# Two kernel edits in a fused stack of mixers: the second half of the down product in other PSUM banks, and the final norm placed ahead of the overflow branch

## What is computed

```python
def swiglu_2(h, w_gate, w_up, w_down):
    a = jnp.einsum("bsd,df->bsf", h, w_gate)
    u = jnp.einsum("bsd,df->bsf", h, w_up)
    return jnp.einsum("bsf,fd->bsd", jax.nn.silu(a) * u, w_down)
...
def second_block(x, mem, ...):
    for l in range(DEPTH):
        ...
        h = rmsnorm_2(x, norm_ffn_w[l])
        if l % 2 == 0:
            x = x + swiglu_2(h, ffn_w_gate[j], ffn_w_up[j], ffn_w_down[j])
        else:
            x = x + moe_swiglu(h, router_w[j], moe_w_gate[j], moe_w_up[j], moe_w_down[j])
    return rmsnorm_2(x, norm_final_w)
```

## Time and profile before

| | us |
|---|---|
| Median of 3 runs | 2752.84 |
| Lowest and highest | 2751.36, 2758.93 |
| The profiled execution, its own time | 2753.78 |
| Its span, from first to last instruction | 2752.0 |
| TensorE busy | 2533.3 |
| VectorE busy | 1757.8 |
| ScalarE busy | 1479.8 |

### The profile page before, as it was taken

The page is one execution under the profiler, slowest core; times in us unless marked ns, Lnnn a source line. Parts: engine busy times, 40 slices in busy tenths (PEclk is TensorE's granted clock), DMA queues, the critical chain, the costliest instruction groups (busy, mean ns, idle before and its releaser), DMA issues.

```text
span 2752.0 us, 42814 instructions
## 1 busy us (share of the span) xinstructions
PE 2533.3 (92%) x17242; PEld 2240.5 (81%) x17242; DVE 1757.8 (64%) x2362; ACT 1479.8 (54%) x1894; POOL 28.0 (1%) x85
## 2 busy tenths in 40 slices
PE   4987799999998789989888999988999999999997
PEld 3865579999997479989688998877788888888886
DVE  3245956545454575546465546556788988988886
ACT  3225545434442564545555435554677777777775
POOL 0000000000000000001000001000000000000000
PEclk8998899999999799999899999999999999999998
DMA  7251415545543164545133455222799999999994
GB/s 275 93 199 61 184 62 199 184 169 184 184 146 143 48 245 169 184 153 185 48 138 139 183 183 172 108 95 106 273 357 349 352 357 353 351 357 352 351 355 181
DMA packets 81580, 566.00 MB, mean 206 GB/s; under 512 B 9265, under 2 KB 12593, under 8 KB 13553
## 3 DMA queue, kind: packets, MB, share of 16 engines
q1 hardware_dynamic: 80096, 559.95, 54.7%
q0 software_dynamic: 1296, 3.38, 0.5%
HBM read 559.92 MB, written 1.05 MB: 204 GB/s over the span
## 4 chain that ended last, share of the span: by engine, by line
PE 82%; DVE 9%; ACT 5%; issue 2%; DMA 1%; SPq 0%; PEldq 0%; DVEq 0%; ACTq 0%
PE psum L232 81%; DVE ring_lo L226 2%; ACT ring_hi L223 1%; PE psum L641 1%; DMA ring<-in_stream 1%; DVE hT L718 1%; PE psum L1829 1%; ACT hT L682 1%; DVE hT L429 1%; DVE Z L1191 1%; ACT Z L690 1%; ACT L415 0%; DVE Z L1165 0%; DVE Z L1164 0%; DVE h_lo L439 0%
## 5 line engine op out<-in xcount | busy, mean ns | idle before, releaser
L226 DVE TENSOR_TENSOR ring_lo<-ring,ring_hi 128x2048 fp32r<-128x2048 f32 x479 | 1096.9, 2291 | 478.4 <-ACT ring_hi L223 475.5
L223 ACT ACTIVATE ring_hi<-ring 128x2048 fp32r<-128x2048 f32 x479 | 916.3, 1914 | 391.0 <-PE psum L232 388.3
L232 PE MATMUL psum<-a_hi,ring_hi 128*128 128x256 f32 (+1 forms) x2448 | 733.0, 299 | 59.7 <-DVE h_lo L437 20.0
L232 PE MATMUL psum<-a_hi,ring_lo 128*128 128x256 f32 (+1 forms) x2448 | 727.0, 297 | 0.0
L232 PE MATMUL psum<-h_lo,ring_hi 128*128 128x256 f32 (+1 forms) x2128 | 629.6, 296 | 0.0
L232 PEld LDWEIGHTS psum<-a_hi,ring_hi 128*128 128x128 f32 x2448 | 476.8, 195 | 77.8 <-issue 43.4
L232 PE MATMUL psum<-ring_hi,a_hi 128*128 128x512 f32 (+1 forms) x1680 | 520.9, 378 | 5.9 <-DVE h_lo L437 3.7
L232 PEld LDWEIGHTS psum<-a_hi,ring_lo 128*128 128x128 f32 x2448 | 476.2, 195 | 10.3
L232 PEld LDWEIGHTS psum<-h_lo,ring_hi 128*128 128x128 f32 x2128 | 415.4, 195 | 7.6
L232 PEld LDWEIGHTS psum<-ring_hi,a_hi 128*128 128x128 f32 x1680 | 313.5, 189 | 58.2 <-issue 4.1
L232 PE MATMUL psum<-ring_lo,a_hi 128*128 128x512 f32 (+1 forms) x976 | 353.3, 362 | 0.0
(11 more groups left out here) (257 smaller groups left out, 2395.7 us busy)
## 6 DMA issues: line engine op xcount, KB each, us to landing
ring<-in_stream SPq DMA_DIRECT2D x529, 1024.0 KB, 4.9
mixT<-mixT POOLq DMA_DIRECT2D x32, 71.0 KB, 5.6
cst<-in_constants SPq DMA_DIRECT2D x1, 1216.0 KB, 14.9
xT<-in_xT SPq DMA_DIRECT2D x1, 1024.0 KB, 9.6
xT<-in_ctxT SPq DMA_DIRECT2D x1, 1024.0 KB, 11.9
xT<-in_memT POOLq DMA_DIRECT2D x1, 1024.0 KB, 6.1
out_y<-hT SPq DMA_DIRECT2D x1, 1024.0 KB, 4.8
Z<-in_level_masks SPq DMA_DIRECT2D x1, 448.0 KB, 15.3
```

Of the source, the lines that this page charges most:

```text
L223: e.activation(hi, raw, ACT.Copy).then_inc(sem("piece_rounded"), 1)
L226: e.tensor_tensor(lo, raw, hi.bitcast(F32), ALU.subtract).then_inc(sem("piece_split"), 1)
L232: ins = pe.matmul(*args, **kw)
```

## The change

Two edits. In the dense feed-forward runs, `ups` and `downs` choose the banks: in runs 0, 2 and 3 the up product stays in banks 0 to 3, half 0 of the down product in 4 to 7, and half 1 goes to 0 to 3; in run 1 all is swapped. The wait for `down_added` goes, and the means that follow some runs move from bank 0 to bank 4. At the end, the last norm is called by each engine ahead of the first `phase_end` behind the experts (and once more inside the branch), the squares are taken two tiles at a time as `e_x_added` rises, the second `phase_end` goes, and the output is stored in two DMAs.

```diff
-        def act_last_norm(act):
-            act_squares(act, 0, T)
-            act_rms(act, 0, 0, T)
-
-        def dve_last_norm(dve):
-            await_next(dve, "inverse_rms")
+        rs_last = hT[:, 0, T:2 * T]
+
+        def pe_last_norm(pe, pre):
             for k in range(KT):
-                dve.scalar_tensor_tensor(hT[:, k, 0:T], xT[:, k, 0:T], v("final2", 0, k, k + 1), mixT[:, 0, 0:T],
-                                         ALU.mult, ALU.mult)
+                if k % 2 == 0:
+                    pe.wait_ge(sem("last_squared"), 4 * (pre == "o") + k // 2 + 1)
+                mm(pe, bank[2][:, 0:T], const("mean"), hT[:, k, 0:T], start=k == 0, stop=k == KT - 1,
+                   last_of="last_mean" if k == KT - 1 else None)
+
+        def act_last_norm(act, pre):
+            act.preload_act_table_set("natural_log")
+            for b in range(4):
+                act.wait_ge(sem(pre + "_x_added"), N_EXP * 4 + b + 1)
+                act.activation(hT[:, 2 * b:2 * b + 2, 0:T], xT[:, 2 * b:2 * b + 2, 0:T], ACT.Square)\
+                   .then_inc(sem("last_squared"), 1)
+            act.wait_ge(sem("last_mean"), 1 + (pre == "o"))
+            link(act, act.activation(rs_last, bank[2][:, 0:T], ACT.Ln, bias=EPS))
+            act.activation(rs_last, rs_last, ACT.Exp, scale=-0.5).then_inc(sem("last_root"), 1)
+
+        def dve_last_norm(dve, pre):
+            dve.wait_ge(sem("last_root"), 1 + (pre == "o"))
+            for k in range(KT):
+                ins = dve.scalar_tensor_tensor(hT[:, k, 0:T], xT[:, k, 0:T], v("final2", 0, k, k + 1), rs_last,
+                                               ALU.mult, ALU.mult)
+                if k % 4 == 3:
+                    ins.then_inc(sem("y_ready"), 1)
...
+        def ups(run):
+            return bank[4:8] if run == 1 else bank[0:4]
+
+        def downs(run, half):
+            return bank[0:4] if (run == 1) != (half == 1) else bank[4:8]
+
...
-                    mm(pe, bank[2 * (f % 2) + half][:, 0:T], w[wp][:, k * 256 + half * P:k * 256 + (half + 1) * P],
+                    mm(pe, ups(run)[2 * (f % 2) + half][:, 0:T], w[wp][:, k * 256 + half * P:k * 256 + (half + 1) * P],
...
                 for d in range(4):
-                    if f == 0 and half == 1:
-                        pe.wait_ge(sem("down_added"), run * 8 + d + 1)
                     for i, (wp, ap) in enumerate(THREE):
                         last = f == FT - 1 and i == 2
-                        mm(pe, bank[4 + d][:, 0:T], w[wp][:, (q % 4) * 512 + d * P:(q % 4) * 512 + (d + 1) * P],
+                        mm(pe, downs(run, half)[d][:, 0:T], w[wp][:, (q % 4) * 512 + d * P:(q % 4) * 512 + (d + 1) * P],
...
-                    ps, x = bank[4 + q % 4][:, 0:T], xT[:, q, off:off + T]
+                    ps, x = downs(run, half)[q % 4][:, 0:T], xT[:, q, off:off + T]
...
-            sp.wait_ge(sem("y_ready"), 1)
-            sp.dma_start(y_out, hT[:, :, 0:T]).then_inc(sem("y_stored"), 16)
-            sp.wait_ge(sem("y_stored"), 16)
+            for half in range(2):
+                sp.wait_ge(sem("y_ready"), half + 1)
+                tiles = slice(4 * half, 4 * half + 4)
+                sp.dma_start(y_out[:, tiles, :], hT[:, tiles, 0:T]).then_inc(sem("y_stored"), 16)
+            sp.wait_ge(sem("y_stored"), 32)
...
                     pe_experts(pe, "e", 0)
+                    pe_last_norm(pe, "e")
                     phase_end(pe)
                     with pe.If(pe.value_load(overflow[0:1, 0:1], min_val=0, max_val=1) > 0):
                         pe_experts(pe, "o", N_EXP // 2)
+                        pe_last_norm(pe, "o")
                     pe.nop()
-                    phase_end(pe)
-            pe_norm(pe, 0, T)
```

More of the change, by code:

```diff
@@ L546, in act_ffn @@
                         act.wait_ge(sem("hidden_full"), run * FT + f - 1)
-                    act.activation(mixT[:, f % 2, 0:T], bank[2 * (f % 2)][:, 0:T], ACT.Silu)\
+                    act.activation(mixT[:, f % 2, 0:T], ups(run)[2 * (f % 2)][:, 0:T], ACT.Silu)\
                        .then_inc(sem("silu"), 1)
@@ L567, in dve_ffn @@
                     dve.wait_ge(sem("silu"), run * FT + f + 1)
-                    dve.tensor_tensor(hid(f, 1, Z), mixT[:, f % 2, 0:T], bank[2 * (f % 2) + 1][:, 0:T], ALU.mult)\
+                    dve.tensor_tensor(hid(f, 1, Z), mixT[:, f % 2, 0:T], ups(run)[2 * (f % 2) + 1][:, 0:T], ALU.mult)\
                        .then_inc(sem("hidden_full"), 1)
@@ L1988, in act_two_norms @@
             await_next(act, "mean_of_normed")
-            act.activation(rs_two[:, 0:T], bank[0][:, 0:T], ACT.Ln, bias=EPS)
+            act.activation(rs_two[:, 0:T], bank[4][:, 0:T], ACT.Ln, bias=EPS)
             link(act, act.activation(rs_two[:, T:2 * T], rs_two[:, T:2 * T], ACT.Ln, bias=EPS * EPS))
@@ L1996, in dve_two_norms @@
             await_next(dve, "two_means")
-            link(dve, dve.tensor_scalar(rs_two[:, T:2 * T], bank[0][:, 0:T], EPS, None, ALU.mult))
-            dve.tensor_tensor(rs_two[:, T:2 * T], rs_two[:, T:2 * T], bank[0][:, T:2 * T], ALU.add)\
+            link(dve, dve.tensor_scalar(rs_two[:, T:2 * T], bank[4][:, 0:T], EPS, None, ALU.mult))
+            dve.tensor_tensor(rs_two[:, T:2 * T], rs_two[:, T:2 * T], bank[4][:, T:2 * T], ALU.add)\
                .then_inc(sem("mean_of_normed"), 1)
@@ L2098, in _ @@
                         load(r * SLOTS + (n_pieces + s - again), (n_pieces + s) % SLOTS)
+                sp.wait_ge(sem("y_ready"), 4)
             sp.nop()
-            sp.wait_ge(sem("y_ready"), 1)
-            sp.dma_start(y_out, hT[:, :, 0:T]).then_inc(sem("y_stored"), 16)
-            sp.wait_ge(sem("y_stored"), 16)
+            for half in range(2):
[3 more added lines that the diff above has]
+            sp.wait_ge(sem("y_stored"), 32)
         @block.tensor
@@ L2126, in _ @@
                 else:
-                    pe_mean(pe, 0, (3, 4, 5, 6, 7), 0, 2 * T, "two_means")
+                    pe_mean(pe, 4, (3, 4, 5, 6, 7), 0, 2 * T, "two_means")
             for layer in range(DEPTH):
@@ L2145, in _ @@
                     pe_ffn(pe, 3)
-                    pe_mean(pe, 0, (3, 4, 5, 6, 7), 0, T)
+                    pe_mean(pe, 4, (3, 4, 5, 6, 7), 0, T)
                 else:
@@ L2194, in _ @@
                 else:
-                    act_rms(act, 0, 0, T)
+                    act_rms(act, 4, 0, T)
                     act_apply(act, [b2_segment("norm_mix", 1)])
@@ L2222, in _ @@
                     act_experts(act, "e", 0)
+                    act_last_norm(act, "e")
                     phase_end(act)
@@ L2225, in _ @@
                         act_experts(act, "o", N_EXP // 2)
+                        act_last_norm(act, "o")
                     act.nop()
-                    phase_end(act)
-            act_last_norm(act)
         @block.vector
@@ L2300, in _ @@
                     dve_experts(dve, "e", 0)
+                    dve_last_norm(dve, "e")
                     phase_end(dve)
@@ L2306, in _ @@
                         dve_experts(dve, "o", N_EXP // 2)
+                        dve_last_norm(dve, "o")
                     dve.nop()
-                    phase_end(dve)
-            dve_last_norm(dve)
-            dve.drain().then_inc(sem("y_ready"), 1)
         @block.gpsimd
```

## The result

| | us |
|---|---|
| Kernel before, median of 4 runs | 2754.06 (2751.36 to 2758.93) |
| Changed kernel, median of 4 runs | 2729.23 (2728.85 to 2732.19) |
| Ratio, changed to before | 0.991, 95% interval 0.9893 to 0.9927 |
| Changed kernel, profiled execution and its span | 2729.36 and 2727.5 |

The change made the kernel faster, by 0.7 to 1.1%. The spans of the two profiled executions differ by 24.5 us.

What follows compares the result with a forecast made beforehand. TensorE, busy 2533.3 of 2752.0 us, was taken to bound the kernel; 8.9 + 3.4 + 9.4 = 21.7 us off the 2752.84 median gave some 2731 us, own range 2726 to 2737, 8 in 10 within 2725 to 2739.

Steps and rivals of the forecast that it cites:

- the predicted 21.7 us: Whole kernel: 8.9 from the middles' waits, 3.4 from the clock behind them, 9.4 from the end.
- 8.9 + 3.4: Dense runs' middles: four TensorE waits of 2.2 us go, and two clock falls of 1.7 us behind them.
- the second claim: Middles: the gain stays, with no later wait for a split; the rival that it is given back had 0.08.
- The lead of 7.3 us: Half 1 of the down product: the next piece is split at 566.9 and wanted at 574.2.
- The end, 9.4: Last norm and store: VectorE ends 9.2 us sooner, TensorE's branch ends last; the gain is 9.4 us.
- 5.1 (4.7 + 0.4): Program end: 4.7 us from VectorE's end to TensorE's drain behind the branch, then 0.4 to the span's end.
- the end costs more: Rival at the end: branch beside the store takes twice, or mean at low clock; 3 to 3.6 us, chance 0.10.
- Storing in two halves alone is worth nothing while the branch is last: Output store: it hides behind TensorE's later branch, so splitting it gains 0 by itself.
- the bound of 10.7: End: upper gain of 10.7 us if the branch costs little, as on ScalarE (45 ns), and the store ends it.
- the trace agrees on ScalarE: Overflow branch: the skill's 0.11 us per compare-and-branch was said to fit ScalarE's 45 ns, not TensorE's 3.63 us.
- the way in which the forecast could fail: Other short stretches: a shift of all work by some us can add or remove a few clock falls.

Runs made afterwards that it cites:

- the first edit alone: Kernel before with only the new banks for the down product and no waits on its additions, end as before: 2737.63 us, ratio 0.9938.
- one store: Changed kernel with a single store of all of hT instead of two; one profiled execution, 7.7 us from VectorE's end to the span's end.
- the two kernels with the new table set: Changed kernel with natural_log_exp_and_others preloaded instead of natural_log: 2712.78 us; the same with phase_end also moved into the overflow branch: 2713.27 us.
- the kernel with the additions first: Kernel before with VectorE's four additions at the middle written ahead of that step's piece split, banks and waits kept: 2739.37 us, ratio 0.9943.
- the two short branches: Changed kernel with a nop instead of the overflow pass: with two stores 3.4 us from VectorE's end to the span's end, with a single store 5.2.
- the early branch: Changed kernel with the phase_end behind the last norm moved into the branch, so TensorE branches right behind its mean products: 2727.75 us, ratio 0.9904.
- the one with new banks: Changed kernel with the four waits on the down product's additions put back, its banks kept: 2745.63 us.
- edit 2: Kernel before with only the last norm ahead of the branch and the two stores, the four waits kept: 2745.24 us, ratio 0.9965.

## Why the prediction was right

**The size.** Forecast 2731, measured 2729.2. Of the predicted 21.7 us the runs gave 12.3 + 9.0 = 21.3 in the two places that were named, and 3.1 more elsewhere in the profiled execution. The medians differ by 24.8 us and not 21.7. That the forecast still lies within 2 us is luck for 1.2 us of it: with a fourth run the median of the kernel before is 2754.06, and I had subtracted from 2752.84.

**The middles, 8.9 + 3.4.** Both terms are right in kind, and 12.3 was measured between the splits, though two small errors cancel in it. An interval with a fall of the clock is 9.6 us and one without is 8.0 to 8.15, so a fall costs 1.5 us, where I had 1.7, and without the falls the pauses cost some 9.3 us, where I had 8.9. That nothing is given back later was the second claim, and the first edit alone shows it. The lead of 7.3 us was more than enough; I did not try how little would do.

**The end, 9.4.** It gave 9.0. The mean took 3.62 us (I had 3.7) at the clock of 1.00. VectorE's end to the span's end was 5.7 us where I had 5.1 (4.7 + 0.4): the flag's load took 0.79 instead of 0.49 us and the branch 4.02 instead of 3.63, both while the store moved. Of the branch's part little is sure: with the DMA engines idle it took 3.4 to 3.9 us. So the rival "the end costs more" was right in its mechanism and took at most 0.6 us, not 3 to 3.6.

**One step was wrong.** "Storing in two halves alone is worth nothing while the branch is last" treated branch and store as independent. The fetch behind the branch shares the DMA engines with the store: with one store the branch takes 2.3 us longer, and the two halves are worth 2.0 us.

**A row misread.** I took the 45 ns of the earlier trace rows as the branch's cost on ScalarE and built the bound of 10.7 on it. ScalarE did nothing for 2.5 us behind that row, so it doesn't show a cheap jump over the long body, and my sentence that the trace agrees on ScalarE doesn't hold for the whole jump. A cheap one is shown only with the short body, 0.24 us on TensorE. The sum did not use it.

**The clock elsewhere.** I named it as the way in which the forecast could fail. It made the kernel faster than my sum has it: the work outside the two places became 3 to 4 us faster in the traces (3.1 us with both edits, 16.2 - 12.3 = 3.9 us with the first edit alone). Behind the last dense run the stretch is 48.3 us in the three traces in which TensorE waited at the middles and 47.4 in the seven in which it did not (the two kernels with the new table set left out here and below); the time at the low clock in it is 6.8 and 3.4 us. Likewise 181.8 to 182.0 against 180.8 us in the stage from 1198 on, in all but the kernel with the additions first, which has 177.7. These two gains came each time that the wait was gone. The 3 us in the stage from 813 on came in the changed kernel, edit 1 alone and the two short branches, and not with one store or the early branch, whose instructions up to there are the same; so it comes and goes from run to run. Why a shift of some us moves a fall was not tried and stays open.

## What to carry to other kernels

Where an engine waits for a short instruction, look at what stands in front of that instruction on its own engine: here four additions of 0.48 us cost 2.2 us because a split of 2.29 us was written ahead of them, and swapping the two took the same 12.3 us from the middles as a second set of banks. Move what the output needs ahead of a rarely taken branch, put the branch itself where no one waits for it, and count a long jump as a DMA that competes with the others. And look for the table load between two functions that alternate: 14 of them were worth 16.5 us here, about as much as the first edit (17.6) and more than the second (10.0).

## What the runs showed that I had not expected

TensorE's branch over the body of the overflow pass took 3.3 to 6.3 us, by what else the DMA engines did. ScalarE's row for it is 45 ns each time, and its stop stands behind the row, 2.4 to 3.8 us in the nine traces in which its next instruction is a drain. TensorE's clock fell behind 5 of the 12 pauses of 2.2 us in the three traces with the wait and behind none of the middles without it. Two falls came in the kernel before and two in the one with new banks, at the same two middles, and one with edit 2 alone, at the second of these. In the kernel before, TensorE had run without a gap ahead of all four pauses, of those with a fall and of those without. What decides between them was not tried.
